# A transformer of four mixers and eight experts: short tasks reordered on TensorE, VectorE and ScalarE in every stage

## What is computed

```python
# first block
x = x + attn_conv_mixer(rms_norm(x), ...)       # windowed attention and a short convolution
x = x + swiglu(rms_norm(x), ...)                # dense, 3584 wide
x = x + recurrent_mixer(rms_norm(x), ...)       # gated linear recurrence
x = x + moe_swiglu(rms_norm(x), ...)            # 8 experts, 3584 wide, top 2 of 8
# second block
for l in range(2):
    h = rmsnorm(x, attn_norm[l])
    q_a, kv_a, g_a, q_b, k_b, v_b, uv_c = jnp.split(h @ w_in[l], IN_OFFSETS, axis=-1)
    o_a = nsa_attention(...)
    o_b = diff_attention(...)
    o_c = chunked_sgu(uv_c, ...)
    gates = jax.nn.sigmoid(h @ w_merge[l] + b_merge[l]).reshape(B, S, 3, D)
    x = x + (gates[:, :, 0] * (o_a @ w_branch_a[l]) + gates[:, :, 1] * (o_b @ w_branch_b[l])
             + gates[:, :, 2] * (o_c @ w_branch_c[l])) @ w_out[l]
    h = rmsnorm(x, ffn_norm[l])
    x = x + (jax.nn.silu(h @ w_ffn1[l]) * (h @ w_ffn3[l])) @ w_ffn2[l]     # 2816 wide
out = rmsnorm(x, final_norm)
```

```python
p = masked_softmax(logits, kpos[None, :] <= t[:, None]).reshape(B, 4, 2, 128, S)
a = p[:, :, 0] - lam * p[:, :, 1]
o = jnp.einsum('bhts,bshe->bthe', a, v)
```

## Time and profile before

| | us |
|---|---|
| median of 3 runs | 2529.75 (2529.59 to 2530.31) |
| profiled execution, whole | 2529.89 |
| profiled execution, span | 2528.1 |
| TensorE busy in the span | 2396.5 (95%) |
| VectorE busy | 1807.5 (71%) |
| ScalarE busy | 1439.1 (57%) |
| data moved by DMA | 586.4 MB, 232 GB/s over the span |

### The profile page before, as it was taken

How to read it: one execution, slowest core, us unless ns; L and a number is a source line. 1 busy time by engine, 2 the same in 40 slices (tenths; PEclk the granted TensorE clock), 3 DMA queues, 4 the chain that set the end, 5 groups by cost and what they waited for, 6 DMA issues and landing times.

```text
span 2528.1 us, 30494 instructions
## 1 busy us (share of the span) xinstructions
PE 2396.5 (95%) x12200; PEld 1990.1 (79%) x12200; DVE 1807.5 (71%) x2402; ACT 1439.1 (57%) x1991; POOL 6.6 (0%) x15
## 2 busy tenths in 40 slices
PE   7999998899999999999999989879999998799998
PEld 6878877687887788788877877669888776698887
DVE  6655457798888888988888886655755567457455
ACT  5344446477777767777777765434444454354443
POOL 0000000000000000000000000000000000000000
PEclk9999999899999999999999999989999999799999
DMA  7355554499999999999999984325555553254551
GB/s 250 114 173 190 177 184 151 152 332 357 326 364 349 351 324 367 348 356 335 363 350 358 336 297 167 117 74 176 167 172 189 167 184 109 75 184 166 176 183 67
DMA packets 277764, 586.40 MB, mean 232 GB/s; under 512 B 9216, under 2 KB 61568, under 8 KB 277616
## 3 DMA queue, kind: packets, MB, share of 16 engines
q1 hardware_dynamic: 276784, 581.82, 65.9%
q0 software_dynamic: 832, 2.56, 0.3%
HBM read 583.30 MB, written 1.05 MB: 231 GB/s over the span
## 4 chain that ended last, share of the span: by engine, by line
PE 84%; DVE 11%; ACT 3%; issue 1%; DMA 0%; DVEq 0%; ACTq 0%; SPq 0%
PE ps L106 80%; DVE low_wlo L121 5%; PE ps L109 4%; ACT low_whi L115 2%; DVE low_hTl L127 1%; ACT L112 0%; DVE low_nv L127 0%; ACT low_hTh L112 0%; DVE low_x L121 0%; ACT low_junk L112 0%; DVE s_p L127 0%; DVE s_p L124 0%; DVE rg_xc L127 0%; DVE low_x L127 0%; ACT rg_ra L112 0%
## 5 line engine op out<-in xcount | busy, mean ns | idle before, releaser
L121 DVE TENSOR_TENSOR low_wlo<-low_raw,low_whi 128x1024 fp32r<-128x1024 f32 (+1 forms) x990 | 1159.6, 1215 | 438.8 <-ACT low_whi L115 438.0
L115 ACT CAST low_whi<-low_raw 128x1024 fp32r<-128x1024 f32 (+1 forms) x990 | 983.8, 1044 | 482.7 <-PE ps L106 480.0
L106 PE MATMUL ps<-low_whi,low_hTh 128*128 128x512 f32 (+2 forms) x1360 | 544.0, 400 | 12.2 <-DVE low_wlo L121 7.4
L106 PE MATMUL ps<-low_wlo,low_hTh 128*128 128x512 f32 (+2 forms) x1360 | 528.8, 389 | 0.0
L106 PE MATMUL ps<-low_whi,low_hTl 128*128 128x512 f32 (+2 forms) x1360 | 528.4, 388 | 0.0
L106 PEld LDWEIGHTS ps<-low_whi,low_hTh 128*128 128x128 f32 x1360 | 262.5, 193 | 60.8 <-DVE low_hTl L127 5.1
L106 PEld LDWEIGHTS ps<-low_whi,low_hTl 128*128 128x128 f32 x1360 | 261.6, 192 | 52.7
L106 PEld LDWEIGHTS ps<-low_wlo,low_hTh 128*128 128x128 f32 x1360 | 262.5, 193 | 45.9 <-issue 0.5
L106 PE MATMUL ps<-low_whi,ffn_Th 128*128 128x512 f32 x608 | 246.5, 405 | 0.0
L106 PE MATMUL ps<-low_wlo,ffn_Th 128*128 128x512 f32 x608 | 240.7, 396 | 0.0
L106 PE MATMUL ps<-low_whi,ffn_Tl 128*128 128x512 f32 x608 | 197.9, 396 | 0.0
(11 more groups left out here) (348 smaller groups left out, 2723.6 us busy)
## 6 DMA issues: line engine op xcount, KB each, us to landing
low_raw<-in_moe_w_down SPq DMA_DIRECT2D x96, 1024.0 KB, 5.5
low_raw<-in_moe_w_gate SPq DMA_DIRECT2D x95, 1024.0 KB, 6.0
low_raw<-in_moe_w_up SPq DMA_DIRECT2D x94, 1024.0 KB, 5.7
low_raw<-in_w_ffn SPq DMA_DIRECT2D x66, 1024.0 KB, 5.0
low_raw<-in_w_in SPq DMA_DIRECT2D x28, 1024.0 KB, 5.3
low_raw<-in_w_merge SPq DMA_DIRECT2D x24, 1024.0 KB, 5.1
raw<-in_moe_w_up SPq DMA_DIRECT2D x18, 1024.0 KB, 6.0
raw<-in_moe_w_gate SPq DMA_DIRECT2D x17, 1024.0 KB, 5.8
```

Of the source, the lines that this page charges most:

```text
L106: return self.real.matmul(*a, **k) if self.real else WALK
L115: return self.real.copy(*a) if self.real else WALK
L121: return self.real.tensor_tensor(*a) if self.real else WALK
```

## The change

Which instructions there are is nearly unchanged (TensorE, SyncE and GpSimd have the same ones); their order on TensorE, ScalarE and VectorE is not.

- `lo_to` and `lo_after` can stop in the middle of a unit. All boundaries but the one into the first Second layer use three common functions:

```diff
             hi_to(e, next_of(name))
 
-        def lo_after(e, name):
-            lo_to(e, next_of(name))
+        def lo_after(e, name, half=1):
+            lo_to(e, next_of(name), half)
 
...
+
+        def act_boundary(e, i, d0, d1):
+
+            act_x(e, i, 0, 0)
+            act_x(e, i, 0, 1)
+            hi_after(e, d0)
+            act_sq(e, i, 0, 0)
+            act_sq(e, i, 0, 1)
+            act_x(e, i, 1, 0)
+            act_x(e, i, 1, 1)
+            act_sq(e, i, 1, 0)
+            act_sq(e, i, 1, 1)
+            hi_after(e, d1)
+
+        def dve_boundary(e, i, d0, d1):
+            dve_residual(e, i, 0, 0)
+            dve_residual(e, i, 0, 1)
+            dve_x(e, i, 0, 0)
+            dve_x(e, i, 0, 1)
+            dve_residual(e, i, 1, 0)
+            lo_after(e, d0, 0)
+            dve_residual(e, i, 1, 1)
+            lo_after(e, d0)
+            dve_x(e, i, 1, 0)
+            dve_norm(e, i, 0)
+            dve_x(e, i, 1, 1)
+            dve_norm(e, i, 1)
+            lo_after(e, d1)
+
+        def pe_begin(e, f, i):
+
+            f.go(e, 0, 0, 2)
+            pe_x(e, i, 1, 0)
+            f.go(e, 0, 2, 5)
+            pe_x(e, i, 1, 1)
+            f.go(e, 0, 5)
 
         def dve_diag(e, i, tb):
 
```

```diff
                         lo_after(e, self.names("d", f - 1)[-1])
+                    if self.i == 1 and f in (1, 3, 4):
+                        (dve_softplus_in, dve_softplus_series, dve_softplus)[(1, 3, 4).index(f)](e)
```

```diff
-                    if x_ and f == 1 and q % 2 == 1:
-                        pe_scatter(e, x_ - 1, q // 4, q // 2 % 2)
-                    if f == 2 and q == 3:
+                    if x_ and f == 1 and q in (2, 6):
+                        pe_scatter(e, x_ - 1, 0, q // 4)
+                    if f == 3 and q == 1:
                         pe_back(e, x_)
-                    if x_ % 2 and x_ < EXPERTS - 1 and f < 4 and q == (4 if f != 1 else 0):
-                        pe_gather(e, x_ // 2 + 1, f)
+                    if x_ % 2 and x_ < EXPERTS - 1 and 2 <= f < 6 and q == 4:
+                        pe_gather(e, x_ // 2 + 1, f - 2)
                 for q in pe_gate_up(e, c_, "u", 1, "mprod"):
-                    pass
+                    if x_ and f == 1 and q in (2, 6):
+                        pe_scatter(e, x_ - 1, 1, q // 4)
                 if c_:
                     for q in pe_down(e, c_ - 1):
...
                     dve_scatter(e, x_ - 1, 0, 1)
-                    lo_after(e, f"{tag}.g{f}.0")
+                if x_ % 2 and x_ < EXPERTS - 1 and 2 <= f < 6:
+                    dve_gather(e, x_ // 2 + 1, f - 2)
+                lo_after(e, f"{tag}.g{f}.1")
+                if x_ and f == 1:
                     dve_scatter(e, x_ - 1, 1, 0)
+                lo_after(e, f"{tag}.u{f}.0")
+                if x_ and f == 1:
                     dve_scatter(e, x_ - 1, 1, 1)
-                lo_after(e, f"{tag}.g{f}.1")
-                lo_after(e, f"{tag}.u{f}.0")
                 dve_prod(e, c_)
```

- End of the experts: the last scatters and the first transposes are interleaved, the first one stands inside the last down product.
- Second layers: the order of the differential blocks. On VectorE and TensorE:

```diff
                 self.dve_dtop(e, 0)
+                self.dve_dw(e, 0)
+                self.dve_dtop(e, 1)
                 lo_after(e, f"{tag}.u.0")
-                self.dve_dw(e, 0)
                 self.dve_dpT(e, 0)
-                self.dve_dtop(e, 1)
+                self.dve_dw(e, 1)
+                self.dve_ob(e, 0)
                 lo_after(e, f"{tag}.u.1")
-                self.dve_ob(e, 0)
-                self.dve_dw(e, 1)
                 self.dve_dpT(e, 1)
```

```diff
                 f.go(e, 0, 4)
-                f.go(e, 1, 0, 4)
+                f.go(e, 1, 0, 2)
+                self.pe_diff(e, 1)
+                f.go(e, 1, 2)
+                f = self.segment("v", 512, ("zv", l))
+                f.go(e, 0, 0, 1)
                 self.pe_dp(e, 0)
-                self.pe_diff(e, 1)
-                f.go(e, 1, 4, 7)
+                f.go(e, 0, 1, 4)
                 self.pe_dav(e, 0)
-                f.go(e, 1, 7)
-                f = self.segment("v", 512, ("zv", l))
-                f.go(e, 0, 0, 3)
+                f.go(e, 0, 4, 6)
+                self.pe_diff(e, 2)
+                f.go(e, 0, 6)
+                f.go(e, 1, 0, 1)
                 self.pe_dp(e, 1)
-                self.pe_diff(e, 2)
-                f.go(e, 0, 3, 6)
+                f.go(e, 1, 1, 6)
                 self.pe_dav(e, 1)
-                f.go(e, 0, 6)
-                f.go(e, 1, 0, 4)
-                self.pe_dp(e, 2)
-                f.go(e, 1, 4, 7)
-                self.pe_dav(e, 2)
-                f.go(e, 1, 7)
+                f.go(e, 1, 6)
                 for z in range(6):
```

More of the change, by code:

```diff
@@ L399, in hi_to, with lo_to @@
                 done["hi"] += 1
-        def lo_to(e, u):
-            while done["lo"] <= u.s:
-                v = split_units[done["lo"]]
-                for h in range(2):
-                    e.wait_ge(*at("hi", v.name, h))
-                    e.tensor_tensor(v.lo[:, v.rows(h), :], v.raw[:, v.rows(h), :],
-                                    v.hi[:, v.rows(h), :].bitcast(F32), SUB).then_inc(*mark("lo", v.name, h))
+        def lo_to(e, u, half=1):
+            while done["lo"] <= 2 * u.s + half:
+                v, h = split_units[done["lo"] // 2], done["lo"] % 2
+                e.wait_ge(*at("hi", v.name, h))
+                e.tensor_tensor(v.lo[:, v.rows(h), :], v.raw[:, v.rows(h), :],
+                                v.hi[:, v.rows(h), :].bitcast(F32), SUB).then_inc(*mark("lo", v.name, h))
                 done["lo"] += 1
@@ L978, in dve_hy @@
             dve_hy_sums(e, "hy_qq", 0, 0, 512)
-            lo_after(e, "hy.q.0")
+            lo_after(e, "hy.q.1")
+            dve_row(e, 0, 0)
+            dve_diag(e, 0, 1)
+            dve_hy_sums(e, "hy_qq", 1, 0, 512)
+            lo_after(e, "hy.q.2")
+            for tb in range(2):
+                dve_hy_sums(e, "hy_kk", tb, 512, 640)
+            dve_hy_heads(e)
+            dve_row(e, 0, 1)
+            dve_hy_c(e, 0)
+            lo_after(e, "hy.kv.0")
             e.wait_ge(*at("d_masks", "in"))
@@ L1144, in act @@
                         hi_after(e, self.names("d", f - 1)[-1])
+                    if self.i == 1 and f == 2:
+                        e.wait_ge(*at("softplus", 0))
+                        e.activation(le, le, AF.Exp, scale=-1.0).then_inc(*mark("rg_le", "all"))
                 i, d = self.i + 1, self.names("d", end)
[L1146 to L1147 removed]
                 if i < 8:
[L1149 to L1157 removed]
+                    act_boundary(e, i, *d)
+                else:
+                    for tb in range(2):
+                        for n in range(2):
+                            act_sq(e, i, tb, n)
             def dve_prod(self, e, f, tb):
```

512 lines of the change are left out of this document (222 added, 290 removed).

## The result

| | before | after |
|---|---|---|
| median us | 2530.03 (4 runs, 2529.59 to 2531.23) | 2411.58 (4 runs, 2411.49 to 2413.20) |
| ratio, with its 95% interval | | 0.9533 (0.9516 to 0.9549) |
| span of the profiled execution | 2528.1 | 2409.9 |
| TensorE idle in it (span less busy) | 131.6 | 55.7 |
| TensorE busy at half clock | 108.2 | 19.9 |

The kernel is 118 us faster (4.7%). The forecast was 2432, with a range of 2408 to 2478: the sign and the range held, and the gain was 20 us larger than the likeliest case; the time is the one that rival (c) had put (2411), though not by (c)'s parts alone, as the last sections say.

A forecast was written before the change was run, and what follows sets the result against it. TensorE was taken as the bound, through its work, waits and half-clock stretches behind long waits. Terms 48.0 + 9.4 + 2.1 + 2.0 + 12.9 + 7.0 + 1.3 + 15.1 = 97.8 us off 2529.9 gave 2432; range 2408 to 2478.

The forecast's parts named there:

- rival (c): Whole kernel: the small new waits put into the forecast don't arise, so 2411 us; chance 0.09.
- the first stages: Attention at the start and boundary to the dense layer: earlier heads and fewer waits gain 12.9 us together.
- the recurrent layer: Boundary, softplus and `rgt_yl` gains less 11.0 us of new waits leave 7.0 us, between 3 and 15.
- the softplus: Recurrent layer: moving it into the dense layer removes the `low_dg` wait and its stretch, gaining 5.0 us.
- The differential attention: Both Second layers: `dve_dw` ahead of the split and later requests by TensorE gain 24.0 us a layer, 48.0 in two.
- the two new waits: Differential attention, each layer: 3.1 us at block 2 with a 1.7 stretch, and 1.9 for `gT` behind `zv`'s gating.
- The boundaries: From a Second layer to its dense layer: residuals first and split halved free 4.7 us each, 9.4 for two.
- a boundary from dense to Second layer: Entry to the second Second layer: 4.7 us freed, VectorE's chain late by 1.3 + 0.7 + 0.5, gain 2.1.
- The experts: Scatters four tiles apart, a split for each, remove seven waits and two half-clock stretches: 15.1 us; 6.7 if VectorE is late.
- (a): Several stages: VectorE takes the place of the waits, hand-overs counted as in time come behind a split; 2476 us, chance 0.22.
- (b): Experts: weights arriving at 346 GB/s bound them, so they keep their 1003 us; 2447 us, chance 0.05.
- (d): Experts' steps: moved scatters and gathers hold up `prod`, making the kernel slower; 2597 us with two splits, chance 0.03.

The follow-up runs named there:

- better: Changed kernel with VectorE's combination of block 2 ahead of a weight split and the norm of zv behind the gates of m0's second half; 2406.92 us.
- better2: Changed kernel with the reorderings of better, plus others at the first Second layer's entry, second transposes, recurrent layer and experts' start; 2402.56 us.
- scatter_old: Changed kernel with the experts' scatters back in their earlier places on TensorE and VectorE, gathers, table and experts' end staying new; 2423.94 us.

## Why the prediction was right, and where its sizes were off

- **What bounds the kernel.** TensorE's waits and its clock, with TensorE's work the same: the two parts of the gain, 75.9 us and 41.5, are nearly the whole of it, and the two runs that share the change between them add up in the waits (76.0 for 75.9). No run takes the first stages (16.9 us), or the new order in the recurrent layer apart from the softplus and the boundary, by themselves; what is said of them below is read from the waits of the two profiles.
- **The differential attention** was the largest term, 48.0, and mis-sized low: the blocks alone gave 54.0 by the medians, and 2 x (20.8 + 9.9 - 3.0) = 55.4 by the rows. The term that was mis-sized is that of the two new waits. I had named both and their causes rightly; they were 1.51 and 1.53 us in place of 3.1 and 1.9, and so short that no stretch at half clock stood behind them, where I had put 1.7. The timelines of the changed kernel show them as they were foretold, each behind one thing on VectorE, a split and the gating of `zv`:

```profile
1604.71 2.36 DVE L121 TENSOR_TENSOR low_wlo<-low_raw,low_whi 128x1024 fp32r<-128x1024 f32 x2 [2.35 <-ACT low_whi L115]
...
1608.76 0.48 DVE L127 SCALAR_TENSOR_TENSOR s_p<-s_p,s_sm,s_p 128x256 f32<-128x256 f32 x1
...
1624.69 1.42 DVE L127 SCALAR_TENSOR_TENSOR s_zv<-s_zv,s_sm,s_sgn 128x512 f32<-128x512 f32 x2
1626.03 0.68 DVE L121 TENSOR_TENSOR s_gT<-ps,low_rb 128x512 f32<-128x512 f32 x1
...
1609.30 0.66 PE L109 MATMUL ps<-low_cst,s_p 128*128 128x128 f32 x4 [1.51 <-DVE s_p L127]
...
1626.77 0.39 PE L106 MATMUL ps<-low_hTh,low_whi 128*128 128x256 f32 x1 [1.53 <-DVE s_gT L121]
```

  VectorE idles 2.35 us ahead of that split, with the combination ready to go; it was this row that `better` was made from.
- **The boundaries** (4.7 each, all of it) came out. Their cause was told short: the old order of residuals and transposes is 1.4 of the 3.0 us, and by the timelines the norm's factor ahead of it the other 1.6. And I had let TensorE's later start and VectorE's order stand as two halves of one remedy; the runs show that either does alone.
- **The last two stretches of the table** hold a boundary from dense to Second layer that I priced at 2.1 since VectorE's chain would be late by 1.3 + 0.7 + 0.5. It was late by 0.91 + 0.77 + 0.32 us, and the stretch at half clock behind the small products in that layer was 3.4 us in place of 6.8. That is 1.6 us which I hadn't counted and which, since the same place has 3.4 or 6.8 in other runs with the code ahead unchanged, I count as luck.
- **The first stages** (12.9 against 16.9): new waits of 1.1, 1.2 and 1.6 us were 0.6, 0.7 and 0.6, and all 3.3 us for `hy_on` and `hy_pT` went, where I had taken 1.0.
- **The recurrent layer** (7.0 against 11.4): the largest of the new waits was right (4.24 for 4.2), the others were 0.8 for 2.1 and 0.5 for 1.1, and those of 0.7 and 1.2 us didn't arise; the stretch behind the largest cost 2.4 in place of 1.7. The softplus's 5.0 was 6.3 by its own run.
- **The experts** (15.1 against 17.0): right in sum, but I gave all of it to the scatters, and 5.8 us go, by the reading above, to the gathers' move, which I had left out.
- **Rivals.** (a), VectorE in the place of the waits: it is busy 41 of 54 us in the differential window and yet not the bound; it shows only in better2. (b) fell: the experts took weights at 353 GB/s. (c) had the right direction and the right time, and the time in part by luck. It let the two new waits of the differential attention vanish (13.4 us), and they stayed, at under half of the price (7.3 gained); of its 21.4 us some 11 came at the places that it named, and the rest in the first stages, the experts, the softplus and the shorter stretch. (d) fell: of the 56 steps of the experts only the very first waits for its product, 1.99 us, and most steps without a gather or a scatter take 17.0 to 17.5 us in both kernels.
- **The table load.** I read from the earlier trace rows that no drain stands between a load and the next instruction. The load shown there can't tell: its next instruction comes 2.42 us behind it. Others in the kernel before can (the load at 407.30 us has the next one 0.01 us behind).
- The chance I gave (c), 0.09, looks too small. Nearly all of my errors have one sign: for a wait that the new order might bring I took the full length of the task in front, though that task has often begun before TensorE asks. The exceptions are new waits that I didn't name, 1.98 and 1.99 us at the start of the experts and 3.27 for 1.30 in the router.

## What to carry to other kernels

Where one engine bounds the time and still idles a little, look at what stands in the helper engine's queue just ahead of the task it waits for: long tasks that nobody waits for belong behind it. At a boundary either a later request or an earlier task was enough; in the differential blocks the later request alone left about a sixth of the loss. Price a wait together with the clock behind it: a boundary's wait of 3.03 us had a stretch at half clock behind it (1.6 us) and one of 1.38 us had none. And read small differences from idle time and the stretches at half clock in the trace, besides the median, when executions of one kernel differ by more than the effect.

## What was not expected of the hardware

- Behind the first 25 us of the fourteen profiles: waits of TensorE of up to 1.6 us that stood alone, some two hundred, had no stretch at half clock behind them; of those of 1.6 to 2.4 us some had one of 3.4 us (one, of 1.94 us with another of 1.32 behind it, had 6.8) and some had none, the wait of 2 us at the first expert among both; those of 2.65 us and more had one each time but one (the wait of 3.3 us at the entry to the first Second layer, which has one in the changed kernel and none in scatter_old). In the router, where waits of 1.5, 1.9, 1.6 and 3.3 us follow each other within 11 us, there is one of 10.2 or 13.7 us. Yet stretches came without a wait too, behind a run of 16 small products, and one and the same place had 3.4 us in one execution and 6.8 in another. How long a wait has to be isn't settled by these runs.
- A table load on ScalarE took 1.28 us and nothing beside in the middle of a busy queue: 14 of the 21 loads in the changed kernel have at most 0.03 us of idle time on either side.
